# Even-layer attention scores as three fp32r matmuls, two query tiles at a time and one position ahead

## The reference, cut to what matters

```python
q = apply_rope(q, cos, sin) * (HEAD_DIM ** -0.5)
k = apply_rope(k, cos, sin)
...
s = jnp.einsum('bhrnqd,bhrnkd->bhrnqk', qs, ks).astype(jnp.float32)
...
s = jnp.where(mask, s, -jnp.inf)
...
p = jnp.exp(s - lse[..., None]).astype(v.dtype)
o = jnp.einsum('bhrnqk,bhrnkd->bhrnqd', p, vs)
```

## Time and profile before

| | |
|---|---|
| median of 3 runs | 1213.33 us (1213.15 to 1213.43) |
| profiled execution, its own time | 1213.26 us |
| its span | 1211.5 us |
| PE busy | 1188.8 us (98%) |
| DVE, ACT, POOL busy | 723.8, 628.0, 681.8 us |
| granted TensorE clock | 0.999 of full speed (2.4 GHz) |

### The profile page before, as it was taken

The page is one execution under the profiler, slowest core; times in us unless marked ns, Lnnn a source line. Parts: engine busy times, 40 slices in busy tenths (PEclk is TensorE's granted clock), DMA queues, the critical chain, the costliest instruction groups (busy, mean ns, idle before and its releaser), DMA issues.

```text
span 1211.5 us, 20288 instructions
## 1 busy us (share of the span) xinstructions
PE 1188.8 (98%) x7714; PEld 1049.2 (87%) x7714; DVE 723.8 (60%) x1368; ACT 628.0 (52%) x1089; POOL 681.8 (56%) x418
## 2 busy tenths in 40 slices
PE   9999999899999999999999999999999999999996
PEld 9877777689999999888888788878999999998885
DVE  2045656449988888612280356553999888872126
ACT  3145646446766666622342467663666666662223
POOL 4543535157877777655534332335587777765453
PEclk9999999999999999999999999999999999999999
DMA  7321121221232222432222121112022223233211
GB/s 283 125 72 73 67 85 70 71 105 36 105 112 106 104 106 103 133 130 77 102 105 107 69 71 69 70 70 104 36 106 104 104 104 104 104 133 110 104 69 70
DMA packets 20041, 117.44 MB, mean 97 GB/s; under 512 B 2448, under 2 KB 2832, under 8 KB 7568
## 3 DMA queue, kind: packets, MB, share of 16 engines
q1 hardware_dynamic: 18400, 112.21, 25.8%
q10 hardware_dynamic: 1584, 4.51, 1.1%
HBM read 110.41 MB, written 2.10 MB: 93 GB/s over the span
## 4 chain that ended last, share of the span: by engine, by line
PE 85%; DVE 8%; ACT 2%; POOL 2%; issue 2%; DVEq 0%; ACTq 0%
PE bank L1491 33%; PE bank L1192 29%; PE bank L1223 14%; POOL w_lo L302 2%; PE bank L1275 2%; PE bank L1302 1%; PE bank L1361 1%; PE bank L1340 1%; PE bank L1289 1%; ACT w_hi L403 1%; DVE ln_mul L810 1%; DVE x L833 1%; PE bank L1350 1%; PE bank L1167 1%; DVE x L790 1%
## 5 line engine op out<-in xcount | busy, mean ns | idle before, releaser
L302 POOL TENSOR_TENSOR w_lo<-w_raw,w_hi 128x1024 fp32r<-128x1024 f32 x116 | 299.1, 2600 | 364.4 <-ACT w_hi L403 353.9
L403 ACT ACTIVATE w_hi<-w_raw 128x2048 fp32r<-128x2048 f32 x55 | 105.2, 1912 | 206.1 <-PE bank L1192 197.5
L1491 PE MATMUL bank<-t_hi,w_hi 128*128 128x256 f32 x640 | 181.3, 283 | 2.6 <-DVE w_lo L1046 2.6
L1491 PE MATMUL bank<-t_hi,w_lo 128*128 128x256 f32 x640 | 181.1, 283 | 0.0
L1491 PE MATMUL bank<-t_lo,w_hi 128*128 128x256 f32 x640 | 181.1, 283 | 0.0
L361 POOL TENSOR_TENSOR w_lo<-w_raw,w_hi 128x512 fp32r<-128x512 f32 x120 | 156.1, 1302 | 20.4 <-ACT w_hi L615 19.5
L1192 PE MATMUL bank<-w_hi,a_hi 128*128 128x512 f32 x480 | 153.4, 395 | 3.2 <-POOL w_lo L302 1.8
L1192 PE MATMUL bank<-w_hi,a_lo 128*128 128x512 f32 x480 | 152.0, 391 | 0.0
L1192 PE MATMUL bank<-w_lo,a_hi 128*128 128x512 f32 x480 | 151.8, 391 | 0.0
L1223 PE MATMUL bank<-xt_hi,w_hi 128*128 128x512 f32 (+1 forms) x416 | 147.1, 354 | 2.4 <-ACT v_all L433 1.7
L1223 PE MATMUL bank<-xt_lo,w_hi 128*128 128x512 f32 (+1 forms) x416 | 147.8, 355 | 0.0
(11 more groups left out here) (130 smaller groups left out, 2508.2 us busy)
## 6 DMA issues: line engine op xcount, KB each, us to landing
w_raw<-w_stream SPq DMA_DIRECT2D x97, 1024.0 KB, 4.8
x<-x_in SPq DMA_DIRECT2D x4, 512.0 KB, 7.5
gain<-ln_in ACTq DMA_DIRECT2D x4, 512.0 KB, 5.8
shift<-ln_in ACTq DMA_DIRECT2D x4, 512.0 KB, 7.1
qs<-qc SPq DMA_DIRECT2D x16, 128.0 KB, 2.0
ks<-kc SPq DMA_DIRECT2D x16, 128.0 KB, 2.0
out<-x SPq DMA_DIRECT2D x3, 512.0 KB, 2.6
w_raw<-w_stream SPq DMA_DIRECT2D x2, 512.0 KB, 6.4
```

Source lines behind the costliest of these rows:

```text
L302: pool.tensor_tensor(w_lo[slot(c)][:, part], w_raw[s][:, part], w_hi[slot(c)][:, part].bitcast(F32), ALU.subtract).then_inc(lo_ready, 1)
L403: act.activation(w_hi[slot(c)][:, :], w_raw[c % 2][:, :], ACT.Copy).then_inc(hi_ready, 2)
L1491: mm = pe.matmul(out, lhs[s][:, at], rhs[:, k, :], start=(k, v) == (0, 0), stop=(k, v) == (3, 2))
```

## The change

Queries and keys of the even layer are split into fp32r high and low parts. A query tile's scores are then three matmuls per head (high by high, high by low, low by high) over all its keys, 128, 256, 384 or 512 columns wide, with the heads alternating. To make the parts, POOL rotates with five operations in place of three, and DVE has two more, in `split_k`. The query tiles 0 and 1 are handled together: one group of scores, one of transposes, one product with the values; and tiles 2 and 3 share one product. The scores of tiles 0 and 1 of the next position are issued at the end of a position. The order on ACT, DVE and POOL changes with it; `heads` moves to the end of a position and takes a step one further on, POOL's `rest` comes after `rotate_q`. The raw and the low parts lie where gain and shift of the layer norm are, whose load moves to the end of the even attention. At the output projection two visits of `beside` change places. The diff, cut:

```diff
+        with ExitStack() as st:
+            qa_lo = [sb(f"qa_lo{s}", [P, S], F32R, stack=st) for s in range(2)]
+            ka_lo = [sb(f"ka_lo{s}", [P, S], F32R, stack=st) for s in range(2)]
+        with ExitStack() as st:
+            qa_raw = [sb(f"qa_raw{s}", [P, S], stack=st) for s in range(2)]
+            ka_raw = [sb(f"ka_raw{s}", [P, S], stack=st) for s in range(2)]
...
+            with ExitStack() as ev:
+                qa_hi = [sb(f"qa_hi{s}", [P, S], F32R, stack=ev) for s in range(2)]
+                ka_hi = [sb(f"ka_hi{s}", [P, S], F32R, stack=ev) for s in range(2)]
...
-                pool.wait_ge(a["q_m"], 2 * i + 2)
-                pool.tensor_tensor(qa[slot][:, :], qc[:, :], qs[:, :], ALU.add).then_inc(a["q_ok"], 1)
+                pool.wait_ge(a["q_m"], 4 * i + 2)
+                pool.tensor_tensor(qa_hi[slot][:, :], qc[:, :], qs[:, :], ALU.add).then_inc(a["q_m"], 1)
+                pool.tensor_tensor(qa_raw[slot][:, :], qc[:, :], qs[:, :], ALU.add).then_inc(a["q_m"], 1)
+                pool.wait_ge(a["q_m"], 4 * i + 4)
+                pool.tensor_tensor(qa_lo[slot][:, :], qa_raw[slot][:, :], qa_hi[slot][:, :].bitcast(F32),
+                                   ALU.subtract).then_inc(a["q_ok"], 1)
                 pool.wait_ge(a["q_ok"], i + 1)
 
             for l in range(DEPTH):
...
                         rotate_q(0, 0)
                 for sname in ("act", "dve"):
                     pool.wait_ge(V[l][sname], NT)
+                if l == 0:
+                    rest(b + AT_QK + 2)
 
                 def position(j, it, dense):
 
                     pool.wait_ge(w_used, b + AT_QK + 2 * it + j + 1)
                     pool.tensor_copy(v_pos[j % 2][:, :, :], v_all[:, :, bass.ds((2 * it + j) * P, P)])\
                         .then_inc(A[l]["v_pos"], 1)
-                    rest(b + AT_QK + 2 + j, it)
                     if l == 0 and dense:
                         rotate_q((j + 1) % 2, 2 * it + j + 1)
+                        rest(b + AT_QK + 3 + j, it)
+                    if l:
+                        rest(b + AT_QK + 2 + j, it)
...
+                exps(0)
+                exps(1)
+                divide(0)
+                divide(1)
+                if before:
+                    out_heads(a, i - 1, (c - 1) % 2)
+                if dense:
+                    act.wait_ge(a["q_mm"], i + 2)
+                    act.activation(qc[:, :], bank[0][:, :], ACT.Copy,
+                                   scale=-MOBA_SCALE).then_inc(a["q_cp"], 1)
+                turned(0)
+                exps(2)
+                divide(2)
+                if dense:
+                    act.wait_ge(w_used, b + AT_QK + i + 2)
+                    act.activation(kc[:, :], bank[1][:, :], ACT.Copy).then_inc(a["k_cp"], 1)
+                turned(1)
+                exps(3)
+                divide(3)
+                if dense:
+                    heads(b + AT_QK + c + 3, it)
+                turned(2)
...
-            load_gain(0)
...
+                if l == 0:
+                    heads(b + AT_QK + 2)
...
+                if l == 0:
+                    load_gain(0)
...
+            def split_k(a, s, i):
+
+                dve.wait_ge(a["k_m"], 4 * i + 3)
+                dve.tensor_copy(ka_hi[s][:, :], ka_raw[s][:, :]).then_inc(a["k_m"], 1)
+                dve.wait_ge(a["k_m"], 4 * i + 4)
+                dve.tensor_tensor(ka_lo[s][:, :], ka_raw[s][:, :], ka_hi[s][:, :].bitcast(F32),
+                                  ALU.subtract).then_inc(a["k_ok"], 1)
 
...
+                bounds(0)
+                bounds(1)
+                divide(0)
+                divide(1)
+                turned(0)
+                bounds(2)
+                divide(2)
+                if before:
+                    out_rests(a, i - 1, (c - 1) % 2)
                 if dense:
                     rope_k_cos(a, (c + 1) % 2, i + 1)
+                turned(1)
+                bounds(3)
+                if dense:
                     rope_k_sin(a, (c + 1) % 2, i + 1)
-                turn_out(a, NT - 1, 0, 4, 4 * i + NT - 1)
+                divide(3)
+                turned(2)
+                if dense:
+                    split_k(a, (c + 1) % 2, i + 1)
...
-                share = (8, 8, 9, 9, 9, 3) if early else (8, 8, 8, 3, 3) if dense else (3, 5, 7, 7, 6)
+                share = (15, 13, 12, 6) if early else (9, 9, 7, 5) if dense else (8, 9, 8, 5)
...
+                def scores(*tiles, p=par):
+
+                    for qi in tiles:
+                        at, L = P if qi == 1 else 0, (qi + 1) * P
+                        for n, (q, k) in enumerate(((qa_hi, ka_hi), (qa_hi, ka_lo), (qa_lo, ka_hi))):
+                            for h in range(2):
+                                part = slice(64 * h, 64 * h + 64)
+                                mm = pe.matmul(bank[2 + h][:, at:at + L], q[p][part, qi * P:(qi + 1) * P],
+                                               k[p][part, 0:L], start=n == 0, stop=n == 2)
+                    mm.then_inc(a["s_mm"], 1)
...
+                    for k in range(tiles[-1] + 1):
+                        q = slice(max(k, tiles[0]) * P, (tiles[-1] + 1) * P)
                         for h in range(2):
                             part = slice(64 * h, 64 * h + 64)
+                            mm = pe.matmul(bank[6 + par][part, q], v_pos[par][:, k, part], probs_t[h][:, k, q],
+                                           start=k == 0, stop=k == tiles[-1])
...
+                if first:
+                    pe.wait_ge(a["q_ok"], i + 1)
+                    pe.wait_ge(a["k_ok"], i + 1)
+                    scores(0, 1)
                 fill(0)
-                for qi in range(NT):
-                    if qi >= 2:
-                        weigh(qi - 2)
-                    if qi + 1 < NT:
-                        pe.wait_ge(a["s_rd"], 8 * i + 2 * qi + 2)
-                        scores(qi + 1)
-                    fill(qi + 1)
-                    turn(qi)
-                weigh(NT - 2)
-                fill(NT + 1)
-                weigh(NT - 1)
+                turn(0, 0, 1)
+                scores(2)
+                fill(1)
+                turn(1, 2)
+                scores(3)
+                weigh(0, 1)
+                fill(2)
+                turn(2, 3)
+                fill(3)
+                weigh(2, 3)
+                if dense:
+                    pe.wait_ge(a["q_ok"], i + 2)
+                    pe.wait_ge(a["k_ok"], i + 2)
+                    scores(0, 1, p=1 - par)
```

More of the change, by code:

```diff
@@ L465, in divide @@
                     act.activation(e, e, ACT.Copy, scale=sm[:, 1, qi % 2, 2:3]).then_inc(a["p_ok1"], 1)
[L467 to L472, removed]
-                for qi in range(NT):
[L475 to L484, removed]
-                    else:
[L486 to L489, removed]
@@ L985, in _ @@
                     rope_k_sin(a, 0, 0)
+                    split_k(a, 0, 0)
                     body = even_body
@@ L1263, in even_position @@
                     more = chain(more, project_early(a, 0, b, c + 2, it))
-                share = (8, 8, 9, 9, 9, 3) if early else (8, 8, 8, 3, 3) if dense else (3, 5, 7, 7, 6)
+                share = (15, 13, 12, 6) if early else (9, 9, 7, 5) if dense else (8, 9, 8, 5)
                 def fill(n):
-                    for _ in range(share[n] if n < len(share) else 0):
+                    for _ in range(share[n]):
                         next(more, None)
-                def scores(qi):
-                    for k in range(qi + 1):
+                def scores(*tiles, p=par):
[7 more added lines that the diff above has]
+                    mm.then_inc(a["s_mm"], 1)
@@ new lines, in turn @@
+                def turn(n, *tiles):
+                    pe.wait_ge(a["p_ok"], 4 * i + tiles[-1] + 1)
+                    pe.wait_ge(a["p_ok1"], 4 * i + tiles[-1] + 1)
+                    if n:
+                        pe.wait_ge(a["tev_v"], 3 * i + n)
+                        pe.wait_ge(a["tev_a"], 3 * i + n)
+                    for h in range(2):
+                        blocks = [(k, qi) for k in range(tiles[-1] + 1) for qi in tiles if k <= qi]
+                        for m, (k, qi) in enumerate(blocks):
+                            mm = pe.transpose(bank[4 + h][:, m * P:(m + 1) * P],
+                                              probs[h][qi % 2][:, k * P:(k + 1) * P], ident[:, :])
+                    mm.then_inc(a["t_mm"], 1)
@@ L1273, in scores, with weigh @@
+                def weigh(*tiles):
+                    if tiles[0] == 0:
+                        pe.wait_ge(a["v_pos"], i + 1)
+                    pe.wait_ge(a["tev_v"], 3 * i + max(tiles[-1], 1))
+                    pe.wait_ge(a["tev_a"], 3 * i + max(tiles[-1], 1))
+                    for k in range(tiles[-1] + 1):
+                        q = slice(max(k, tiles[0]) * P, (tiles[-1] + 1) * P)
                         for h in range(2):
                             part = slice(64 * h, 64 * h + 64)
```

(19 more changed lines are left out.)

66 lines of the change are left out of this document (26 added, 40 removed).

## The result

The changed kernel took 1241.23 us (median of 4, 1240.52 to 1241.32), the kernel before 1213.38 on the same chip: ratio 1.0228, 95% interval 1.0215 to 1.0241. It is slower by 28 us. The forecast was 1218 with a range of 1206 to 1227: the sign was right, the size was wrong by 23 us, and the measured time lies outside the range. The profiled execution has a span of 1239.5 us. Behind position 7 the two kernels run alike: from where PE's chain enters the last run of output matmuls to the end it is 976.9 us (from 262.59), and 977.2 before (from 234.35, with two matmuls more). So the whole loss, 28 us of span, lies in front of that point.

A forecast was written before the change was run, and what follows sets the result against it. PE set the pace before; after, blocked DVE and POOL stretches would. 76.35 + 20.6 + 105.5 + 22.1 + 14.9 = 239.45 against 234.85 before, 4.6 us longer: 1213.3 + 4.6 = 1218, range 1206 to 1227.

The forecast's parts named there:

- the end of the position: After tile 3: only DVE's subtraction waits for POOL's first `rest`, until 20.3; PE stalls 0.7, position 21.1 us.
- the rule: On DVE and POOL: a two-input DVE operation or division waits for POOL's current operation; POOL's next takes 0.34 us more.
- position 0: First even position: no predecessor's output to copy, so 20.6 us.
- positions 1 to 5: Middle even positions: 21.1 us each against 20.4 before, together 105.5 us.
- position 6: Fewer fillers before turn(2, 3), so k is copied only at 11.6 and others queue behind: 22.1 us against 18.5 before.
- The stall before the transposes of tiles 2 and 3: PE waits 1.9 us for ACT's division, as `rope_k_sin` precedes `divide(3)` and its sum waits for POOL's fifth operation.
- POOL's rotation: Five operations of 1.28 us where there were three, beginning at about 6.6 and ending at 13.0 at best.
- PE's own work: PE's work per dense position falls from 20.4 to about 18.6 us, by 1.1 and 0.7.
- Rival D: Scores: row halves don't work side by side in fp32r, 1.6 us more scores a position, total 1227; chance 0.20.
- Rival B: `rope_k_sin` and `split_k`: waits fall into slack, PE stays the bound at 18.6 us a position, total 1202; chance 0.13.
- Rival C: Only one of the two DVE waits bites; with only `split_k`'s 19.5 us a position, total 1208; chance 0.20.

The follow-up runs named there:

- experiment 1: Changed kernel with split_k moved ahead of turned(2) on DVE: 1221.83 us, ratio 1.0075.
- experiment 2: Changed kernel with POOL waiting for k_ok of the next position before it starts `rest`: 1225.04 us, ratio 1.0099.
- experiment 3: Changed kernel with four additions of 10 columns on POOL before `rest`, results never read: 1226.42 us, ratio 1.0116.
- experiment 4: Changed kernel with one addition of 40 columns on POOL before `rest`, result never read: 1228.48 us, ratio 1.0124.
- experiment 5: Changed kernel with twelve unread fp32 matmuls of 128 columns ahead of PE's wait for k_ok: 1244.69 us, ratio 1.0263.
- experiment 8: experiment 2 with divide(3) ahead of `rope_k_sin` on DVE: 1215.16 us, ratio 1.0015.
- experiment 7: experiment 1 with position 6's fillers shared 12, 12, 1, 5 in place of 9, 9, 7, 5: 1220.92 us, ratio 1.0065.
- experiment 9: experiment 8 with position 6's fillers shared 12, 12, 1, 5 as in experiment 7: 1210.34 us, ratio 0.9978.
- experiment 10: Changed kernel without low parts (three matmuls on high parts), divide(3) ahead of `rope_k_sin`, position 6's fillers 12, 12, 1, 5: 1203.5 us, ratio 0.9922.

## Why the prediction was wrong in size

**The step that failed** is the end of the position: "casts ka_hi until 17.55 (half of 0.683), and its subtraction comes 0.1 us after POOL has taken over". In the same clock (t = 0 at 99.18, where position 1's scores(0, 1) are done) the rows say: ACT's division ended at 15.4 (forecast 15.5), the transposes began at 15.8 (15.6), POOL began `rest` at 17.3 (17.4), DVE came to its cast at 17.5 (17.2). These terms were right within 0.3 us, but the forecast had the cast ahead of POOL by 0.2 us, less than the error of the terms, and it came behind by 0.18. From there the sum splits: k_ok at 22.7 for 20.3. The forecast used the rule that the later of the two waits for the whole operation of the other, for DVE operations with two inputs and divisions, as its rows showed it. It applied the rule to the subtraction and not to the cast. Extended to the cast, and with the order turned, the rule gives the measured schedule: POOL's first `rest` until 19.8, the cast 0.3 later, the subtraction behind the second `rest` at 22.7, a position of 23.6 us, and 23.75 was measured. The other order was not priced. Experiments 1 to 4 show the cause from both sides. The Trainium skill (SBUF — State Buffer, Who interferes with whom) says that issue order decides who blocks, and counts casts among the DVE instructions that can take part; experiment 4's rows agree with both.

**The clock had no term at all.** The forecast priced its waits at their length. Behind them the granted clock was 0.87 to 0.93 in five positions; experiment 5 puts this at 0.96 us in a position like 2 to 4.

**Where the 23 us are**, forecast against found: before position 0, 1.5, of which 1.0 is two waits of PE at 36.56 and 38.90 for POOL's `rest`, pushed back by the longer first rotation (the forecast had no place for it); position 0, 0.8; positions 1 to 5, 14.9 (120.44 for 105.5), of which some 10 is the blocked cast in four of them (2.4 each), 3 to 4 the clock (an estimate, four positions at the 0.96 of experiment 5); position 6, 4.2 (26.33 for 22.1); position 7, 1.7, with waits of 0.5 to 1.1 us before each of its transposes. That makes 23.1; the split of positions 1 to 5 leaves 1 to 2 us that no single row accounts for.

**Position 6** was forecast as the worst, and was: k's copy ended at t = 13.0 for 11.6, and the block came on top. The clock isn't the reason for the late copy: the fillers in front of it started 0.23 us apart. What came late is PE, by two waits:
```profile
222.82 0.85 PE L1350 MATMUL bank<-ident,probs 128*128 128x128 f32 x6 [0.41 <-ACT probs L482]
227.88 0.88 PE L1350 MATMUL bank<-ident,probs 128*128 128x128 f32 x6 [1.22 <-DVE probs L957]
```
With fewer fillers in front, PE was at the transposes before the divisions were done. It had passed those of tile 2 at t = 9.1, where the forecast said 7.8, and scores(3) at 9.9 for 8.5: that is the 1.4 us. In experiment 1 the two waits are the same, and so is the copy's end. Without the block (in experiment 1 cast and subtraction took 0.42 and 0.69 us there) it still took 24.7 to 25.1 us in experiments 1, 2 and 8, 2.6 to 3.0 over the forecast; experiments 7 and 9 take 2.1 and 4.2 us off by projecting k earlier.

**What held.** The stall before the transposes of tiles 2 and 3: forecast 1.9, found 1.9 and 1.6 in positions 0 and 1, where the clock had not fallen yet, and 1.5 to 1.6 in positions 1 to 5 of experiment 1. Its cause (both operations of `rope_k_sin` ahead of the division, behind POOL's rotation until t = 14) is shown by experiment 8, which removed it for 9.9 us. POOL's rotation began at t = 6.7 (6.6) and its five operations ended at 14.0. PE's own work fell, to 18.95 us (18.6). Rival D is out; the six matmuls of 512 columns:
```profile
108.64 0.50 PE L1336 MATMUL bank<-ka_hi,qa_hi 64*128 64x512 f32 x2
108.97 0.39 PE L1336 MATMUL bank<-ka_lo,qa_hi 64*128 64x512 f32 x2
109.21 0.39 PE L1336 MATMUL bank<-ka_hi,qa_lo 64*128 64x512 f32 x2
109.53 0.87 PE L1364 MATMUL bank<-probs_t,v_pos 128*64 128x256 f32 x8
```
From 108.64 to 109.53 is 0.89 us with two changeovers, a pair every 0.23 or so: side by side. Rival B's 18.6 us a position is only approached without the split (18.95 in experiment 10). Rival C, one wait of the two, was priced with that of `split_k` alone, 19.5 us a position, and no run has that; experiment 1 leaves the other one alone, and takes 20.7.

**What stays open**: which waits of some 2 us lower the clock. One of 1.88 us in position 0 left it up in experiment 1, and one of 1.90 at the same place lowered it in experiments 2 and 7; but in experiment 5 one of 2.01 us lowered it and one of 2.07 did not. The outcome is worth 1 to 2 us in the total, as much as some of the differences here. (The lowered clock of position 6 in experiments 9 and 10 stands behind longer waits, 2.71 and 2.31 us.)

## What to carry to other kernels

Where two engines exclude each other, as DVE and POOL do here, and both are released by the same event, work out who comes first and by how much; if the margin is smaller than the error of the sum, the forecast has two values (here 21 and 23.6 us a position) and both belong in the range. Such a meeting is better ordered by hand: a wait on the engine that is not urgent (POOL, experiment 2) won 16 us and made PE wait for no weights in the even positions. An operation that several others wait for, here the division, goes ahead of one that may itself be blocked. And when PE stops setting the pace, a wait costs more than its length, since the clock may fall behind it.

## What the runs showed of the hardware

- A DVE cast of 512 columns from fp32 to fp32r takes 0.42 us alone and is blocked by a running POOL operation like one with two inputs (up to 2.64 us); a lead of 0.03 to 0.08 us was enough for it to go first (changed kernel, experiment 4). POOL is blocked in the same way (additions of 10 columns: 0.20 us alone, 0.65 behind DVE's subtraction), and between two short POOL operations DVE gets in.
- Score matmuls of half height pair up on PE whether the heads alternate or not: three pairs of 512 columns start 0.33 to 0.34 and then 0.22 to 0.24 us apart in both orders.
- After idles of 2.2 to 5.4 us in the even positions PE's fillers started 0.42 to 0.43 us apart in place of 0.23, at once or a few fillers later; after idles of 1.85 to 2.07 us they did so in some cases and not in others.
